# Four edits to a two-block transformer kernel: order of a projection, place of a softplus, a split rotary, and the pitch of the weight ring

## The reference

```python
def first_block(x, ...):
    for i in range(2):
        x = layer_norm(ALPHA * x + 0.5 * swiglu(x, ffn_w_in[i, 0], ffn_w_out[i, 0]))   # 1024 -> 2 x 2816 -> 1024
        x = layer_norm(ALPHA * x + token_mix(x, mix_w_in[i], ..., mix_w_out[i]))
        x = layer_norm(ALPHA * x + 0.5 * swiglu(x, ffn_w_in[i, 1], ffn_w_out[i, 1]))
        x = layer_norm(ALPHA * x + sigmoid(x @ ple_w_gate[i] + b) * (p[i] @ ple_w_proj[i]))

def token_mix(h, w_in, ..., w_out):
    # h @ w_in is cut into: stick-breaking attention (4 heads of 64), a gated delta rule
    # (4 heads of 128, chunks of 64 tokens, q, k, v behind a causal convolution, q and k
    # of unit length, output RMS-normed and gated by silu(z)), a short convolution (256 wide)
    return concat([o_sb, o_gdn, o_sc]) @ w_out      # 256 + 512 + 256 rows of w_out

def second_block(x, ...):
    for l in range(2):
        c_q, c_kv, k_r, gate_a, q_d, k_d, v_d, gate_b, gates = split(x @ w_in[l])
        # a: latent attention, q and k from RMS-normed c_q, c_kv; b: differential attention
        q_b, k_b = rotary(q_d), rotary(k_d)         # rotates 16 of each 64 channels
        y_a = (attention(q_a, k_a, v_a) * silu(gate_a)) @ w_branch_a[l]
        y_b = (rms_norm(diff_attention(q_b, k_b, v_d)) * silu(gate_b)) @ w_branch_b[l]
        g = sigmoid(gates + b_merge[l])
        x = layer_norm(ALPHA * x + (g[:, :1024] * y_a + g[:, 1024:] * y_b) @ w_out[l])
```

## Time and profile before

| | before |
|---|---|
| median of 3 runs | 1508.51 us (1508.16 to 1509.04) |
| profiled execution, its own time | 1506.74 us |
| its span | 1504.9 us |
| mean granted clock of PE | 0.998 |
| PE busy | 1490.7 us, 99% |
| DVE busy | 943.8 us, 63% |
| ACT busy | 816.1 us, 54% |
| POOL busy | 217.7 us, 14% |
| instructions | 27364 |

### The profile page before, as it was taken

One profiled execution on the slowest core, in us unless ns is written; L12 is line 12 of the kernel. 1 busy time (PEld: TensorE's weight loads), 2 busy tenths in 40 slices (PEclk: granted clock), 3 DMA queues, 4 the chain that ended last, 5 costly groups with the idle time before them and its releaser, 6 DMA issues.

```text
span 1504.9 us, 27364 instructions
## 1 busy us (share of the span) xinstructions
PE 1490.7 (99%) x11622; PEld 1378.5 (92%) x11622; DVE 943.8 (63%) x1382; ACT 816.1 (54%) x1259; POOL 217.7 (14%) x127
## 2 busy tenths in 40 slices
PE   9999999999999999999999999999999999999998
PEld 8999899989998889998899989998789999899997
DVE  6655466676555475655557675655477767667756
ACT  6554366645454365554476554554375675555762
POOL 0000152113000261000432040000430001400001
PEclk9999999999999999999999999999999999999999
DMA  9655464326555456555553155555455334553341
GB/s 384 230 194 188 155 221 141 99 99 236 185 196 197 165 205 225 195 189 187 196 182 118 67 186 199 195 196 194 170 210 196 113 141 159 206 186 137 129 152 56
DMA packets 39720, 266.26 MB, mean 177 GB/s; under 512 B 4460, under 2 KB 4716, under 8 KB 9392
## 3 DMA queue, kind: packets, MB, share of 16 engines
q1 hardware_dynamic: 38304, 260.13, 49.1%
q0 software_dynamic: 720, 3.35, 0.6%
q10 hardware_dynamic: 576, 1.05, 0.2%
HBM read 263.46 MB, written 1.05 MB: 176 GB/s over the span
## 4 chain that ended last, share of the span: by engine, by line
PE 93%; DVE 4%; ACT 2%; issue 1%; DMA 0%; SPq 0%; ACTq 0%; DVEq 0%
PE PS L487 17%; PE PS L488 17%; PE PS L489 17%; PE PS L501 6%; PE PS L503 6%; PE PS L502 6%; PE PS L562 4%; PE PS L559 4%; PE PS L560 4%; PE PS L470 1%; PE PS L471 1%; PE PS L472 1%; PE PS L614 1%; PE PS L1954 1%; PE PS L1351 1%; PE PS L1968 1%
## 5 line engine op out<-in xcount | busy, mean ns | idle before, releaser
L487 PE MATMUL PS<-xTH,WH 128*128 128x256 f32 x2256 | 640.9, 284 | 0.0
L488 PE MATMUL PS<-xTL,WH 128*128 128x256 f32 x2256 | 628.3, 278 | 0.0
L489 PE MATMUL PS<-xTH,rawL 128*128 128x256 f32 x2256 | 626.3, 278 | 0.0
L319 DVE TENSOR_TENSOR rawL<-raw,WH 128x1024 fp32r<-128x1024 f32 (+1 forms) x408 | 491.5, 1231 | 112.9 <-ACT WH L316 112.4
L316 ACT ACTIVATE WH<-raw 128x1024 fp32r<-128x1024 f32 (+2 forms) x476 | 484.6, 1048 | 129.9 <-PE PS L562 101.3
L487 PEld LDWEIGHTS PS<-xTH,WH 128*128 128x128 f32 x2256 | 423.6, 188 | 9.0 <-issue 6.6
L488 PEld LDWEIGHTS PS<-xTL,WH 128*128 128x128 f32 x2256 | 423.7, 188 | 3.4 <-issue 2.9
L489 PEld LDWEIGHTS PS<-xTH,rawL 128*128 128x128 f32 x2256 | 424.7, 188 | 0.0
L319 POOL TENSOR_TENSOR rawL<-raw,WH 128x1024 fp32r<-128x1024 f32 (+1 forms) x68 | 162.5, 2413 | 766.4 <-ACT WH L316 766.4
L316 ACT ACTIVATE sg<-PS 128x256 f32<-128x256 f32 x79 | 30.4, 384 | 177.8 <-PE PS L489 177.8
L319 DVE TENSOR_TENSOR hh<-PS,sg 128x256 f32<-128x256 f32 x79 | 33.5, 424 | 144.9 <-ACT sg L316 144.9
(11 more groups left out here) (366 smaller groups left out, 2010.6 us busy)
## 6 DMA issues: line engine op xcount, KB each, us to landing
raw<-in_weights SPq DMA_DIRECT2D x233, 1024.0 KB, 4.8
gb<-in_lngb SPq DMA_DIRECT2D x16, 512.0 KB, 5.1
raw<-in_weights SPq DMA_DIRECT2D x2, 1056.0 KB, 4.9
gb<-in_ln SPq DMA_DIRECT2D x4, 512.0 KB, 4.4
cst<-in_consts POOLq DMA_DIRECT2D x1, 1378.5 KB, 10.3
x0T<-in_xT ACTq DMA_DIRECT2D x4, 256.0 KB, 5.7
raw<-in_weights SPq DMA_DIRECT2D x4, 256.0 KB, 5.3
xt<-in_x POOLq DMA_DIRECT2D x1, 1024.0 KB, 17.3
```

The costliest lines, as they stand in the source:

```text
L319: return Q.put(eng, waits, lambda e: e.tensor_tensor(out, a, b, op))
L487: e.matmul(out, c, xTH[:, k, :], start=k == 0, stop=False)
L488: e.matmul(out, c, xTL[:, k, :], start=False, stop=False)
L489: ins = e.matmul(out, u.L(i, 128 * k, 128), xTH[:, k, :], start=False, stop=k == KD - 1)
```

## The change

1. `CHW` is 1024 instead of 1056, so that WH slots lie 4096 bytes apart; `over` and all tiles above the ring move down by 1 KB. The lead unit mix_va comes in three chunks (k 0 to 2, 3 to 5, 6 and 7; 792, 792 and 528 columns) instead of two of 1056.
2. `MIX_ORDER` takes k 2 and 3 of the delta rule before k 6 and 7 of the short convolution.
3. `sb_soft(1)` is issued behind the second chunk of the delta rule, ahead of two reductions of `rms`, instead of behind them.
4. In `rotary`, w is written as fp32r, DVE makes its remainder wl from PSUM (`lo`), the permutation is two fp32r matmuls with a copy of the matrix in fp32r (`permR`, by ACT), the cosine product reads PSUM, and the sine product has a tile of its own.
5. The values of the latent attention (`vat`) take their banks of PSUM from ring B instead of A.

```diff
-CHW = 1056
+CHW = 1024
...
-            units.append((("mix_va", l), [[(*w, kt, [(512, 256), (2816, 8)]) for kt in range(4 * c, 4 * c + 4)] for c in range(2)]))
+            units.append((("mix_va", l), [[(*w, kt, [(512, 256), (2816, 8)]) for kt in kts] for kts in VA_KTS]))
...
-MIX_ORDER = [0, 1, 6, 7, 2, 3, 4, 5]
+MIX_ORDER = [0, 1, 2, 3, 6, 7, 4, 5]
+VA_KTS = [range(0, 3), range(3, 6), range(6, 8)]
...
-            for c in range(2):
-                def fn(e, c=c):
-                    for q in range(4):
-                        k = 4 * c + q
+            for c, kts in enumerate(VA_KTS):
+                def fn(e, c=c, kts=kts):
+                    for q, k in enumerate(kts):
...
-                p = pe([u.ready(c, 0), xT_ready[t][c], free], fn)
+                p = pe([u.ready(c, 0), xT_ready[t][kts[0] // 4], xT_ready[t][kts[-1] // 4], free], fn)
...
-        fill = [lambda: sb_scores(0), lambda: sb_scores(1), lambda: go(1), lambda: (go(1), sb_soft(1), sb_sums(0)), lambda: sb_sums(1),
+        fill = [lambda: sb_scores(0), lambda: sb_scores(1), lambda: go(1), lambda: (go(1), sb_sums(0)), lambda: sb_sums(1),
...
                 if c == 1:
+                    sb_soft(1)
                     rms(0)
                     rms(1)
...
-        rw = [put_at("rwa", [128, 2, S], 36), put_at("rwb", [128, 2, S], 38)]
+        rw = [put_at("rwa", [128, 2, S], 36, F32R), put_at("rwb", [128, 2, S], 38, F32R)]
+        rl = [put_at("rla", [128, 2, S], 70, F32R), put_at("rlb", [128, 2, S], 72, F32R)]
+        rs_, permR = put_at("rsum", [128, 2, S], 74), put_at("permR", [128, 128], 76, F32R)
...
+        perm_ready = act(permR[:, :], C("perm"), ACT.Copy, [xw])
...
-            w = rw[i]
+            w, wl = rw[i], rl[i]
             a = act(w[:, :, :], v2(b), ACT.Copy, [p, rw_free[i]])
-            release(b, a)
-            c = tt(pr[:, :, :], w[:, :, :], two(C("dcos")), ALU.mult, [a, pr_free[0]])
+            lo = tt(wl[:, :, :], v2(b), w[:, :, :].bitcast(F32), ALU.subtract, [a])
+            c = tt(pr[:, :, :], v2(b), two(C("dcos")), ALU.mult, [p, pr_free[0]])
+            release(b, a, lo, c)
...
-                p2 = pe([a, free], lambda e: e.matmul(PS[:, b2, :], C("perm"), w[:, :, :].rearrange("p j s -> p (j s)"), start=True, stop=True))
-                s = tt(w[:, :, :], v2(b2), two(C("dsin")), ALU.mult, [p2, c])
+                def fn(e):
+                    e.matmul(PS[:, b2, :], permR[:, :], w[:, :, :].rearrange("p j s -> p (j s)"), start=True, stop=False)
+                    return e.matmul(PS[:, b2, :], permR[:, :], wl[:, :, :].rearrange("p j s -> p (j s)"), start=False, stop=True)
+                p2 = pe([perm_ready, a, lo, free], fn)
+                s = tt(rs_[:, :, :], v2(b2), two(C("dsin")), ALU.mult, [p2, c])
                 release(b2, s)
-                y = tt(dst, pr[:, :, :], w[:, :, :], ALU.add, [s, c])
+                y = tt(dst, pr[:, :, :], rs_[:, :, :], ALU.add, [s, c])
...
         vat = []
         for t in range(2):
-            b, free = bank("A")
+            b, free = bank("B")
```

## The result

The changed kernel takes 1495.88 us in the median of four runs (1493.67 to 1497.95), the kernel before 1508.72 us beside it: a ratio of 0.9915, interval 0.9903 to 0.9928. The profiled execution took 1497.95 us, with a span of 1496.2.

What follows compares the result with a forecast made beforehand. PE was taken to bound the kernel, busy 1490.7 us of a 1504.9 us span. The terms -2.6 - 0.8 - 1.6 - 3.2 + 2.6 sum to -5.6 us, giving a median of 1502.9 us, range 1499.0 to 1507.2.

Steps and rivals of the forecast that it cites:

- Order of the projection: Mixer's output projection: starting its second group with k 2, 3 ends PE's wait for scL, -2.6 us for two layers.
- sb_soft(1): PE's wait for ez at L1503: issuing it ahead of two DVE reductions ends the wait, -0.8 us for two layers.
- Rotary: Four rotaries per layer: fp32r permutations save 0.40 us each, but the first waits for lo, +0.40; -1.6 us in all.
- Three lead chunks: Shifted chunk numbers put POOL's shared rawL before sqa, so PE waits: +2.6 us for two layers, between 0 and +4.0.
- Slots 4 KB apart: Weight slots alike modulo 256 remove the odd slots' slower chunks: -3.2 us, between -3.5 and 0.
- the odd slots' extra: Chunks in odd slots take longer: 0.037 us over 36 row-product chunks (1.3 us), 0.033 us over 57 stationary ones (1.9 us).
- 107 slow chunks and 175 fast ones: Stationary-weight chunks: 107 at the slow pace differ by slot by 0.033 us; 175 in later units take 2.72, no difference.
- Rival C: Eight slots alike modulo 4 KB hinder each other, fast chunks lose 0.10 us each: up to 1523.6 us; chance 0.05.
- Rival A: Weight slots: the distance between them does nothing, so -2.4 us in all, 1506.1 us; chance 0.22.
- Rival B: Squares in the mixer: POOL's order does not bite, no wait for sqa, so -8.2 us, 1500.3 us; chance 0.20.

Runs made afterwards that it cites:

- The second measurement: The changed kernel run once more, unedited, against the kernel before: 1499.06 us (1497.74 to 1499.21), ratio 0.9936.
- e3: The changed kernel with the old slots, 4224 bytes apart, and two lead chunks again: 1504.03 us, ratio 0.9972 to the kernel before.
- e1: The kernel before with only the lead weights in three chunks, slots still 4224 bytes apart: 1509.59 us, ratio 1.0014.
- e2: The kernel before with three lead chunks and slots 4096 bytes apart, nothing else: 1501.25 us, ratio 0.9956.
- e7: The changed kernel with all eight weight slots (upper halves) moved by 128 bytes to 64 modulo 256, lower halves left at 192: 1521.7 us.
- e11: The changed kernel with squares issued earlier (1493.26 us), plus tokens' tiles at 192 modulo 256 instead of 128: slower by 36 us than without that move.
- e15: The changed kernel with squares issued earlier and transposes after unit 4, plus all weights at 0 modulo 256, tokens at 128; median not in the text, 1517 to 1529 us expected.
- e9: The kernel before with each ffn's transposes after unit 4 instead of unit 8: 1504.95 us, ratio 0.9976.
- e13: The changed kernel with squares issued earlier (1493.26 us), plus tokens moved to 192 and all weights to 0 modulo 256: 1503.2 us.
- e8: The changed kernel with slots 4160 bytes apart, so at 192, 0, 64 and 128 modulo 256 in turn: 1523.3 us.

## Why the prediction was wrong

The direction was right, the size was not. The second measurement, 1499.06 us, would have lain just inside the range, but by the luck of the pace: its profile, too, has three of four early ffn stretches fast. Taken step by step:

**Order of the projection, -2.6: right.** In e3, where nothing else changes PE's pace there, PE gains 1.27 and 1.29 us from the projection to the next ffn in the two layers. In the changed kernel the group starts without a wait, with gH:

```profile
324.89 0.60 PE L1575 MATMUL PS<-cst,on 128*128 128x128 f32 x4
325.25 0.48 PE L503 MATMUL PS<-WH,gH 128*128 128x512 f32 x1
325.56 0.40 PE L504 MATMUL PS<-rawL,gH 128*128 128x512 f32 x1
```

**sb_soft(1), -0.8: wrong, about -0.1.** In e3 the stretch gains 0.06 and 0.02 us. The wait for ez is gone, but the sums' second head now waits for a bank of PSUM; the timelines of PE and of ACT in the changed kernel:

```profile
301.96 0.49 PE L1504 MATMUL PS<-ez,cst 128*128 128x128 f32 x2 [0.25 <-ACT rsa L318]
...
303.05 1.16 PE L1629 MATMUL PS<-vn,kdec 64*128 64x128 f32 x8
```

```profile
300.89 0.30 ACT L318 ACTIVATE small<-small,cst 64x4 f32<-64x4 f32 x1 [0.18 <-DVE small L1561]
301.22 0.20 ACT L318 ACTIVATE small<-small 64x4 f32<-64x4 f32 x1
301.33 0.57 ACT L318 ACTIVATE rsa<-PS 128x512 f32<-128x512 f32 x1
```

The reductions that were moved back on DVE feed small operations on ACT; the copy rsa, which frees that bank, stands behind these in ACT's queue and ends at 301.90. The prediction followed DVE's and PE's queues and not the third one. L1629 starts at 303.05, where 303.00 stood.

**Rotary, -1.6: right.** In e3's layer 0, at one pace, PE is 0.39 us later one unit after the first rotary and 0.81 us ahead after all four. The first wait is the one foretold: lo of DVE ends at 1131.85 + 0.69 = 1132.54 and PE starts 0.14 later. The profile puts this wait down to ACT's crs, the first of which ends at 1132.63; but in the changed kernel PE starts 0.15 behind lo as well (1127.91 and 1128.06), before the first crs ends there (1128.23).

```profile
1131.85 0.69 DVE L319 TENSOR_TENSOR rla<-PS,rwa 128x512 fp32r<-128x512 f32 x1 [0.20 <-ACT rwa L316]
```

```profile
1132.68 0.47 PE L1812 MATMUL PS<-rwa,permR 128*128 128x512 f32 x1 [0.57 <-ACT crs L316]
1132.99 0.40 PE L1813 MATMUL PS<-rla,permR 128*128 128x512 f32 x1
```

**Three lead chunks, +2.6: right in its mechanism, short in size, 3.6.** POOL's rawL took 3.39 us beside DVE's, 1.01 more than the 2.38 of the earlier trace rows; the prediction weighed this case (1.2 us more, 2.0 in all) and went by 1.3. PE stood ready at 221.47 - 1.57 = 219.90, 1.4 us before the 221.28 of the earlier trace rows. POOL's Eu began 1.15 us earlier as well (215.79 against 216.94), so only some 0.3 us of that, from k chunks that had become faster, lengthens the wait. In layer 1 a wait of 0.4 us for sqb comes on top.

**Slots 4 KB apart, -3.2: the step that failed; -8.3 measured (e1 to e2).** Its small part, the odd slots' extra, held: row products run at 2.75 in all slots, slow stretches at 2.83. What failed is the sentence that counted 107 slow chunks and 175 fast ones and took this division as given. It is not: the same matmuls have two paces, and at the new distance three early ffn stretches went over to the faster one, 1.65 us each, with parts of the mixer and the last gates, while 20 chunks of the second block went the other way. Rival C saw that a chunk can change its pace and knew the price, 0.10 us, but only asked it in one direction. The trace of the kernel before held a hint: between the earlier trace rows the slow stretch ends at the transposes, at 59.31 us. Rival A falls: e7, e11 and e15 change nothing but addresses against their base kernels and move the time by 23 to 36 us. With it falls what the prediction drew from the rule of the Trainium skill ("SBUF — State Buffer", "SBUF: two separate sides"), that the distance is worth nothing. Whether TensorE waits for another user of SBUF there, or its own two operands hinder each other, no run tells. Rival B falls in the changed kernel, whose PE waits 3.1 us for sqa.

The parts measured alone add up to -8.3 (slots), +1.5 (lead chunks) and -4.1 (the rest, with four chunks of the second block slow that were fast before), -10.9 us; the two measurements of the whole are -12.8 and -9.7 (1499.06 against 1508.72). Within what the pace leaves uncertain, this closes. It stays open what settles the pace at the start of a stretch, and why one distance is better than another; the runs show only which of the distances tried are good here, and that other work between the matmuls can change the pace, to the fast one in e9, to the slow one in three ffn phases of e7 and in ffn(0, 0) of e13.

## What to carry to other kernels

Before a stretch that is bound by PE is called full, compare the steps of equal instructions in it: two values for the same matmul mean that the slower one may be avoidable, and small moves of tiles, or of the work between, are a cheap trial. When a piece of work is moved in one queue, follow every queue that its result enters up to the banks that are freed there. Numbering that decides which engine takes a piece is part of an edit that changes the count of pieces.

## What the runs showed of the hardware that was not expected

The pace of PE's fp32r matmuls with 256 moving columns changed with the distance, counted modulo 256 bytes, between the weights and the moving operand. In the ffn phases 24 of them took 2.72 or 2.83 us at 64 bytes, 2.72 or 2.85 with the upper halves at -64, 2.85 at 128 and 2.88 at 0, at one granted clock of 0.998 to 0.999. Other distances were tried only by turns (e8, 2.83). Where two paces occur, a stretch mostly keeps the one that it has; in the kernel before and in e9 the slow pace ended at the transposes, or one unit behind them. POOL's subtraction beside DVE's took 3.39 us, where it takes 2.38 alone; DVE's took 1.64 us there, no more than beside POOL's Eu alone (1.65).
